# Router logits inside the norm stage, a shorter routing chain, and routing joined with the experts, in a two-layer transformer kernel

## What is computed

```python
grp_p = softmax(xt @ w_grp + b_grp)                    # 4 groups
grp_prob, grp_idx = top_k(grp_p, 1)
e_logits = (xt @ w_rt + b_rt).reshape(-1, 4, 4)[group chosen]
top_p, top_i = top_k(softmax(e_logits), 2)             # 2 experts of 4
top_w = grp_prob * top_p / sum(top_p)
y = sum over chosen experts of top_w * ((silu(xt @ wg) * (xt @ wu)) @ wd)
h = layer_norm(ALPHA * h + y)
```

## Time and profile before

| | |
|---|---|
| Median of 3 runs | 3097.36 us (3094.57 to 3097.85) |
| The profiled execution | 3095.71 us |
| Its span, first to last instruction | 3093.9 us |
| TensorE busy | 2519.2 us, 81% of the span |
| VectorE busy | 1262.1 us, 41% |
| ScalarE busy | 969.2 us, 31% |
| GpSimd busy | 783.3 us, 25% |
| Mean granted TensorE clock | 0.894 |

### The profile page before, as it was taken

One profiled execution on the slowest core, in us unless ns is written; L12 is line 12 of the kernel. 1 busy time (PEld: TensorE's weight loads), 2 busy tenths in 40 slices (PEclk: granted clock), 3 DMA queues, 4 the chain that ended last, 5 costly groups with the idle time before them and its releaser, 6 DMA issues. The chain is left out here.

```text
span 3093.9 us, 34445 instructions
## 1 busy us (share of the span) xinstructions
PE 2519.2 (81%) x12970; PEld 1955.7 (63%) x12970; DVE 1262.1 (41%) x2642; ACT 969.2 (31%) x1543; POOL 783.3 (25%) x224
## 2 busy tenths in 40 slices
PE   6996888666993887994899378986999878896998
PEld 4774777555771675663676346755887747675886
DVE  3524555355444315756543544042022262222122
ACT  2322111222441114761343224241222333332222
POOL 2430000223332320012243211313443202224441
PEclk8997999887996996997999688998999988998999
DMA  3350000133883234112586411212322202223221
GB/s 103 106 205 7 1 1 1 41 110 117 279 270 112 86 84 132 49 54 83 179 282 219 151 44 41 94 57 59 135 96 77 85 28 69 69 69 99 96 82 61
DMA packets 220636, 304.40 MB, mean 98 GB/s; under 512 B 51938, under 2 KB 139508, under 8 KB 220484
## 3 DMA queue, kind: packets, MB, share of 16 engines
q1 hardware_dynamic: 218196, 294.18, 29.1%
q0 software_dynamic: 2304, 8.39, 0.8%
HBM read 270.97 MB, written 31.56 MB: 98 GB/s over the span
## 5 line engine op out<-in xcount | busy, mean ns | idle before, releaser
L158 POOL TENSOR_TENSOR branch_weights_wl<-branch_weights_wf,branch_weights_wh 128x2048 fp32r<-128x2048 f32 (+1 forms) x66 | 301.2, 4564 | 791.5 <-ACT branch_weights_wh L152 791.5
L152 ACT ACTIVATE branch_weights_wh<-branch_weights_wf 128x2048 fp32r<-128x2048 f32 (+1 forms) x66 | 125.0, 1894 | 418.4 <-PE bprojc_acc L200 132.8
L1401 POOL TENSOR_TENSOR rt_wl<-rt_wf,rt_wh 128x2048 fp32r<-128x2048 f32 x34 | 173.8, 5113 | 294.2 <-ACT rt_wh L1397 294.2
L200 PE MATMUL merge_acc<-xh,branch_weights_wh 128*128 128x512 f32 x384 | 153.4, 399 | 19.1 <-PEq L71 19.1
L200 PE MATMUL merge_acc<-xh,branch_weights_wl 128*128 128x512 f32 x384 | 151.9, 395 | 0.0
L200 PE MATMUL merge_acc<-xl,branch_weights_wh 128*128 128x512 f32 x384 | 150.8, 393 | 0.0
L158 POOL TENSOR_TENSOR nsa_weights_wl<-nsa_weights_wf,nsa_weights_wh 128x2048 fp32r<-128x2048 f32 x13 | 60.1, 4625 | 297.8 <-ACT nsa_weights_wh L152 297.6
L1528 PE MATMUL exp_ps_y<-rt_wf,exp_ht 128*128 128x512 f32 x256 | 118.9, 608 | 3.7 <-ACT exp_ht L1567 3.7
L1397 ACT ACTIVATE rt_wh<-rt_wf 128x2048 fp32r<-128x2048 f32 x64 | 121.8, 1907 | 0.0
L1507 PE MATMUL exp_ps_gu<-rt_wh,exp_xh 128*128 128x512 f32 x256 | 113.1, 442 | 0.0
L1491 PE MATMUL exp_ps_xh<-exp_pick,xh 128*128 128x256 f32 x512 | 87.0, 293 | 29.9 <-DVE exp_pick L1607 27.1
(11 more groups left out here) (601 smaller groups left out, 6439.5 us busy)
## 6 DMA issues: line engine op xcount, KB each, us to landing
branch_weights_wf<-w_in SPq DMA_DIRECT2D x56, 1024.0 KB, 4.9
rt_wf<-moe_w_gate SPq DMA_DIRECT2D x64, 512.0 KB, 6.9
rt_wf<-moe_w_up SPq DMA_DIRECT2D x64, 512.0 KB, 7.9
rt_wf<-moe_w_down SPq DMA_DIRECT2D x32, 1024.0 KB, 6.3
in_weights_wf<-gdn_w_in SPq DMA_DIRECT2D x16, 1024.0 KB, 5.5
moe_rows<-exp_y SPq DMA_DIRECT2D x32, 512.0 KB, 3.0
moe_rows<-gproj_zeros SPq DMA_DIRECT2D x1, 12288.0 KB, 35.9
merge_bwf<-w_branch SPq DMA_DIRECT2D x12, 1024.0 KB, 5.1
```

What stands on the lines that cost most here:

```text
L152: act.activation(self.h[u][:, :, 0:self.cols(b)], self.s.f[u][:, :, 0:self.cols(b)], ACT.Copy).then_inc(self.s.hi_ready, 1)
L158: pool.tensor_tensor(self.l[u][:, :, 0:self.cols(b)], self.s.f[u][:, :, 0:self.cols(b)], self.h[u][:, :, 0:self.cols(b)].bitcast(F32), ALU ...
L200: mm = pe.matmul(self.acc[:, s, 0:cols], lhs[:, P * s:P * s + P], rhs, start=(u == 0 and k == 0 and n == 0), stop=(u == 1 and k == HALF - ...
L1401: eng.tensor_tensor(self.l[b][u][:], self.f[b][u][:], self.h[b][u][:].bitcast(F32), ALU.subtract).then_inc(self.lo_ready[u], 1)
```

## The change

- **Router logits in the norm stage.** A class `Logits` loads and splits the router weights in `stage_out_norm`. For each tile TensorE multiplies with the tokens as weights of the array and the 20 router columns moving, behind a wait for that tile's low part. Logits of tile t - 2 stand between the product of tile t and the turn of tile t - 1; those of tiles 2 and 3 stand ahead of and behind the last turn. The result stays in `g.logits`.
- **Turn** uses a ring of 3 single banks there instead of 4.
- **A shorter chain.** No full softmax: comparisons work on differences of logits, exponentials are taken beside the chain, and the weights come after it. The counting uses 8 small float32 matmuls that accumulate in one bank, and fewer VectorE instructions behind them.
- **One stage.** `stage_route` is gone; class `Route` does its work inside `stage_experts`, in parts: `slots` (up to the row numbers), `tables` behind the first `x_lo`, `weights` behind `choose(1)`. Weight loads start behind the small loads. `last_pair` waits for the table and is read behind the first two blocks on the engines that run them.
- **Low part of h** moves from GpSimd to VectorE, between `choose(0)` and the first `x_lo`. VectorE also takes unit 0 of the first block's weight split; GpSimd does unit 1 of blocks 0 and 1 once the low part of `h` is there.
- **spin**: TensorE multiplies 128x512 float32 into a bank that nobody reads, three times ahead of the counting and four times behind it.

```diff
@@ stage_out_norm, TensorE
                 for t in range(TT):
                     out.second_block(pe, t)
+                    if t >= 2:
+                        logits.pe(pe, t - 2)
                     if t:
                         pe.wait_ge(norm.done, t)
                         turn.pe(pe, t - 1)
+                logits.pe(pe, TT - 2)
                 pe.wait_ge(norm.done, TT)
                 turn.pe(pe, TT - 1)
+                logits.pe(pe, TT - 1)
@@ class Logits
+    def pe(self, pe, t):
+        if t == 0:
+            pe.wait_ge(self.lo, 1)
+        for half in range(2):
+            pe.wait_ge(self.turn.lo_done, 2 * t + half + 1)
+            for k in range(HALF * half, HALF * half + HALF):
+                for m, (x, w) in enumerate(((self.g.xh, self.wh), (self.g.xl, self.wh), (self.g.xh, self.wl))):
+                    mm = pe.matmul(self.acc[:, 0, self.n * t:self.n * t + self.n], x[:, k, P * t:P * t + P], w[:, k, :],
+                                   start=(k == 0 and m == 0), stop=(k == KT - 1 and m == 2))
+        mm.then_inc(self.done, 1)
@@ class Route
+    def pe(self, pe):
+        pe.wait_ge(self.onehot, 1)
+        oh = self.oh16
+        pe.matmul(self.ps[:, 0, 0:64], self.g.striu[:], oh[:].rearrange("p t e -> p (t e)"), start=True, stop=False)
+        for t in range(TT - 1):
+            pe.matmul(self.ps[:, 0, 16 * (t + 1):64], self.g.ones[:],
+                      oh[:, t:t + 1, :].to_broadcast([P, TT - 1 - t, N_EXP]), start=False, stop=(t == TT - 2))
+        for t in range(TT):
+            mm = pe.matmul(self.ps[:, 0, 64:80], self.g.ones[:], oh[:, t, :], start=(t == 0), stop=(t == TT - 1))
+        mm.then_inc(self.counted, 1)
@@ stage_experts, SyncE
+                route.load(sp)
                 sp.dma_start(iota[:], a["c_iota"]).then_inc(ld, 16)
+                ws.load_first(sp)
                 end = last_pair(sp)
@@ stage_experts, TensorE
-                end = last_pair(pe)
+                def spin(calls):
+                    for _ in range(calls):
+                        pe.matmul(ps_y[:, 0, :], g.ident[:], g.h[:, 0, 0:512], start=True, stop=True)
+                spin(3)
+                route.pe(pe)
+                spin(4)
@@ gather
-                    for kk in (2 * part, 2 * part + 1):
-                        k = HALF * v + kk
-                        for src, dst in ((rt.hh, ps_xh), (rt.hl, ps_xl)):
+                    for src, dst in ((rt.hh, ps_xh), (rt.hl, ps_xl)):
+                        if first(j) and part == 0:
+                            pe.wait_ge(*((h_hi, TT) if src is rt.hh else (h_lo, TT * (v + 1))))
+                        for kk in (2 * part, 2 * part + 1):
+                            k = HALF * v + kk
@@ stage_experts, ScalarE
-                end = last_pair(act)
+                for t in range(TT):
+                    act.activation(rt.hh[:, t, :], g.h[:, t, :], ACT.Copy).then_inc(h_hi, 1)
+                route.act(act)
...
+                for u in range(2):
+                    ws.hi(act, 0, u, 1)
                 x_hi(0, 0)
@@ stage_experts, GpSimd
+                pool.wait_ge(h_lo, 2 * TT)
+                for b in range(2):
+                    ws.lo(pool, b, 1, b + 1)
                 end = last_pair(pool)
-                ws.lo(pool, 1, 1, 2)
@@ stage_experts, VectorE
-                end = last_pair(dve)
+                route.slots(dve)
...
                 choose(0)
+                for v in range(2):
+                    cols = slice(512 * v, 512 * v + 512)
+                    for t in range(TT):
+                        if v == 0:
+                            dve.wait_ge(h_hi, t + 1)
+                        dve.tensor_tensor(rt.hl[:, t, cols], g.h[:, t, cols], rt.hh[:, t, cols].bitcast(F32),
+                                          ALU.subtract).then_inc(h_lo, 1)
+                ws.lo(dve, 0, 0, 1)
                 x_lo(0, 0)
                 x_lo(0, 1)
+                route.tables(dve)
                 choose(1)
+                route.weights(dve)
                 for t in range(TT):
                     ins = dve.tensor_scalar(g.h[:, t, :], g.h[:, t, :], ALPHA, None, ALU.mult)
```

More of the change, by code:

```diff
@@ L1091, in stage_out_norm @@
         out, norm = OutProduct(g, st, run), LayerNorm(g, st, gain, shift)
-        turn, ws = Turn(g, st, g.h), out.ws
+        turn, ws = Turn(g, st, g.h, 3), out.ws
+        logits = Logits(g, st, a, layer, turn)
         with nc.Block() as block:
@@ L1096, in _ @@
                 ws.load_rest(sp)
+                logits.load(sp)
                 norm.load(sp)
@@ L1130, in take @@
                     norm.stats(dve, t, b)
+                logits.split(dve)
                 for t in range(TT):
@@ L1139, in _ @@
                 turn.lo(dve, TT - 1)
+                logits.take(dve, g.logits)
 def stage_ffn_norm(g, name, gain, shift, nxt, pre_gain):
@@ L1200, with __init__ @@
 MAX_BLOCKS = MORE_BLOCKS + N_EXP
[L1203 to L1217, removed]
+class Route:
+    def __init__(self, g, st, a, rt, ps):
+        self.g, self.a, self.rt, self.ps = g, a, rt, ps
@@ new lines, in __init__ @@
+        self.ohs, self.oh16, self.pos, self.past = small("ohs", 4), small("oh16", 16), small("pos", 16), small("past", 16)
+        self.f = st.sb("f", [P, 2, TT, N_EXP])
+        self.blocks, self.incl, self.base, self.one16 = (st.sb(x, [P, N_EXP]) for x in ("blocks", "incl", "base", "one16"))
+        self.over = st.sb("over", [P, N_EXP, TT - 1])
+        self.sg, self.le, self.more = small("sg", 1), st.sb("le", [1, MORE_BLOCKS, N_EXP]), st.sb("more", [1, MORE_BLOCKS // 2])
+        self.tabf = st.sb("tabf", [1, MAX_BLOCKS + 1])
@@ new lines, in __init__, with load @@
+        self.loaded, self.step, self.g_diff, self.second, self.exps = (st.sem("r_" + x) for x in
+            ("loaded", "step", "g_diff", "second", "exps"))
+        self.onehot, self.counted, self.tabled = st.sem("r_onehot"), st.sem("r_counted"), st.sem("r_tabled")
+    def load(self, sp):
+        a, ld = self.a, self.loaded
+        sp.dma_start(self.desc[:], rows_of(a["c_desc"], 0, N_GRP)).then_inc(ld, 16)
+        sp.dma_start(self.thr[:], rows_of(a["c_thr"], 0, TT - 1)).then_inc(ld, 16)
+        sp.dma_start(self.place[:], bass.AP(a["c_place"].tensor, a["c_place"].offset,
+                                            [[0, P], [N_EXP, 2], [1, N_EXP]])).then_inc(ld, 16)
+        sp.dma_start(self.iota_b[:], a["c_iota_b"]).then_inc(ld, 16)
@@ L1639, in _ @@
                 ins.then_inc(scaled, 1)
-                pairs(dve, end, body)
+                end = pairs(dve, body)
                 dve.wait_ge(y_stored, end * 32 + 32)
-                dve.tensor_copy(slot[:, 0, 0:1], slot[:, 0, 1:2]).then_inc(added, 1)
+                dve.tensor_copy(slot[:, 0, 0:1], slot[:, 1, 0:1]).then_inc(added, 1)
                 dve.wait_ge(scaled, 1)
```

284 lines of the change are left out of this document (133 added, 151 removed).

## The result

The changed kernel takes 3061.07 us (median of 4, 3057.78 to 3064.96), the one before 3095.97 in the same comparison: a ratio of 0.9888 (95% interval 0.9871 to 0.9905). The prediction was 3042, with a range of 3030 to 3061: right in sign, wrong in size. 34.9 us were gained where 55.0 were summed. The profiled execution took 3060.98, with a span of 3059.2 and a mean granted clock of 0.898.

What follows compares the result with a forecast made beforehand. Between norm stage and first expert matmul, VectorE held off by GpSimd was taken as costing 16 us per layer. Savings 30.4 + 29.5 - 4.3 - 0.6 = 55.0 gave 3097.4 - 55.0 = 3042 us, range 3030 to 3061.

Steps and rivals of the forecast that it cites:

- norm stage longer: End of the norm stage: router logits there add 5.4 us in layer 0 and 6.2 in layer 1.
- S to one-hots: Joint stage's first DMA (S) to the one-hots: load wait 3.4 us plus eighteen VectorE instructions 4.0.
- counting: Eight float32 matmuls on TensorE behind the one-hots: 3.9 us per layer, taken at half clock.
- S to P: Joint stage's first DMA (S) to the first pick (P): 17.4 us per layer.
- P to G: First pick (P) to first expert matmul (G), low part of h now on VectorE: 12.45 us per layer.
- block 0 longer: First expert block: hid 9.2 us after the first expert matmul, TensorE waits 2.15 us; last_pair adds 0.3 per layer.
- rival C: Norm stage's end: logits dearer or at half clock, half clock in last turn; +4 us per layer, 3050; chance 0.10.
- rival A: Block 0: GpSimd's split cuts into VectorE's scaling of h, delaying hid; 6.4 us per layer, 3055; chance 0.28.
- S to G: Joint stage's first DMA to the first expert matmul: 29.85 us per layer.
- Rival B: 5.05 us after the first pick: GpSimd's weight split goes ahead of VectorE's; +4.5 us per layer, 3051; chance 0.07.
- The spins: TensorE's unread products ahead of and behind the counting: second costs nothing and should give the gather full clock.
- D: The spin keeps TensorE's clock up through the counting: 2 us less per layer, 3038; chance 0.08.

Runs made afterwards that it cites:

- e7: Changed kernel with high and low router weights side by side, 40 columns at once, 16 matmuls per tile instead of 24: 3048.71 us.
- e9: Like e7, but each of the 16 matmuls of a tile moves 128 columns, at most 40 of them used: 3047.73 us.
- e3: Changed kernel with the last turn put ahead of the logits of tile 2: 3054.18 us.
- e2: Changed kernel with GpSimd's split of block 1 made to wait for the end of the scaling of h: 3051.15 us.
- e1: Changed kernel with the scaling of h moved between VectorE's two copies of xl: 3040.79 us.
- e6: Changed kernel with eight 128x512 float32r filler products ahead of the logits of tile 2: 3051.07 us.
- e14: Changed kernel with an unused tile of 192 bytes per partition, no instruction differing: 3078.65 us.
- e16: Changed kernel with an unused tile of 256 bytes per partition, no instruction differing: 3061.45 us.
- e5: Changed kernel with the low part of h moved back from VectorE to GpSimd: 3067.06 us.
- e13: Kernel before the change with an unused tile of 320 bytes per partition, no instruction differing: 3079.19 us.
- e4: Changed kernel with both spins left out: 3048.77 us.
- e15: Changed kernel with the edits of e1, e3 and e7, three routing loads made in the norm stage, five fillers and an unused 64-byte tile: 3009.11 us.

## Why the prediction was wrong

Of the 55.0 us, 26.7 are there in *touched*; 8.0 of the 34.7 between the two spans were gained in stages that the diff doesn't touch. The error of the sum is therefore 28 us and not 20: a missing term hid part of it. The steps below add up to 28.8.

| step (us per layer, layer 0 / 1) | predicted | measured | error of both |
|---|---|---|---|
| norm stage longer | 5.4 / 6.2 | 13.0 / 13.8 | 15.2 |
| stage change | 1.2 | 1.2 / 1.2 | 0 |
| S to one-hots | 7.4 | 8.8 / 8.1 | 2.1 |
| counting | 3.9 | 3.8 / 2.4 | -1.6 |
| S to P, with the above | 17.4 | 18.6 / 16.6 | 0.4 |
| P to G | 12.45 | 13.8 / 12.4 | 1.3 |
| block 0 longer | 2.45 | 8.4 / 8.4 | 11.9 |

(The norm stage in layer 0: 659.32, where the logits of tile 1 take the place of the turn, to 677.69, against 661.43 to 669.39 before, 10.4 more, and 2.6 for tile 0. In layer 1 it is 11.2 and 2.6 in the same way.)

*Norm stage: the step that failed most.* Two parts of it. The price of a matmul was taken as 0.08 us and is 0.111, above the bound of 0.10; the nearest row, the transposes of 128 columns, was read as 0.1 and then lowered. In that same row they start every 0.109 us at full clock (661.43, 661.54, 661.65), and the last eight every 0.213 at half, so both prices stood there. e7 and e9 show that columns have no part in it. And "TensorE now idles less before it, so I take full clock in both" was wrong: both layers were at half clock from the logits of tile 2 to the end (rows at 664.55 and 672.12), and e3 shows that such matmuls let the clock fall without any gap. That is rival C, with a chance of 0.10 and 4 us per layer; it cost 7.6. About 2 of these are the price (0.03 us for each of 72 matmuls on the path), the rest is the clock. The order also cost: with the turn first (e3) 4.7 us per layer come back.

*Block 0: rival A.* "`hid` comes at 9.2" holds only with GpSimd away (e2: 9.09). The rival had the mechanism, the place (13.6, measured 13.39) and the price (6.4 per layer over the forecast, measured 6.0) right, and a chance of 0.28 that was too small. The argument against it, that the overlap is only the last two of four instructions, didn't help: GpSimd asked during the third and got in ahead of the fourth, and one gap between two instructions is enough. By the Trainium skill (SBUF — State Buffer, "SBUF: two separate sides") two such instructions of VectorE and GpSimd exclude each other for a whole instruction, and the trace agrees (the fourth scaling was held for 4.3 us), but no row of before had shown GpSimd winning against a queue of VectorE's. Rivals A and C together, priced as on record, would have made 3042 + 12.8 + 8 = 3063; the range left the pair out as a doubled mishap, though nothing makes them exclude each other.

*S to G was right* within 1.7 us over both layers, by terms that err against each other: the four loads took 4.9 and 4.2 us after S, above the bound of 4, and the counting in layer 1 ran mostly at full clock (mean 0.82), which was luck: with the same instructions there e1, e2, e3, e6, e7, e14 and e16 took 3.6 us for it and 30.6 to 33.6 from S to G. The clean chain was right: no routing instruction over 0.4 us, and e5 shows that this is what the moved subtraction bought. So was the moved subtraction's cost. Rival B fell: VectorE starts first, at 702.36, and GpSimd's 6.51 us hold its wait.

*The spins* were costed at nothing and credited with a warm gather. The gather did start at clock 1.00, but it then waits for the low part of `h`, and in layer 0 its second half was at 0.55 all the same. D didn't happen in layer 0 and half in layer 1.

*What no step named* is where tiles lie. By e13 and e14 it is worth 18 us of the 34.9 by medians (19 and 13 by the ratios), 10 to 12 us by *rest*. The logic of the change by itself is the ratio of changed to e13, 0.9888 / 0.9939 = 0.9949 or 16 us, and that of e14 to before, 0.9931 or 21 us. With their intervals these agree with each other and, within 10 us, with *touched*. Not settled is a part of what *rest* varies by among kernels with good places (2345.7 to 2358.4): one attention stage took 67.3 us in the changed kernel's profile and 60.1 in that of e4, at mean granted clocks of 0.75 and 0.84, and no instruction of it differs.

## What to carry to other kernels

When work of one engine is put ahead of an instruction on which the bottleneck waits, ask not only how long it is but whether another engine that shares its SBUF access can get in between two of its instructions: the price is then the other one's whole instruction, here 4.3 us and a TensorE at half clock. Small matmuls with fresh weights are priced by the weights (0.111 us each), they let the clock fall here even where TensorE was never idle, and they don't belong ahead of the turn on which the chain waits. And before a gain of under 1% is credited to a change that allocates a tile, the kernel before should be timed with the same tile and nothing else.

## What was not expected of the hardware

- An unused tile of 320 bytes per partition makes the kernel before 18 us faster (0.9939); 128x512 float32r matmuls of an unchanged stage go from a mean of 399 to 394 ns. 256 bytes more change nothing, 192 more undo it.
- The granted clock fell to half inside 7.32 us, and twice inside 19.20 us, in which TensorE was busy without a gap, during matmuls of 20 columns with new weights each.
- A matmul with new 128x128 weights costs 0.111 us at full and 0.213 at half clock with 20, 40 or 128 moving columns.
- GpSimd gets its turn between two back-to-back VectorE instructions: four scalings of 2.49 us took 6.80, the fourth alone 4.98. VectorE's copy of `xl` from PSUM (704.56, 1.22 us) was not held, though GpSimd's split ran from 702.52 to 709.03.
- The fastest kernel of this study, e15, takes 3009.11 us, 0.9706 of the one before (0.9688 to 0.9724).
